# Order of TensorE's products in the split feed-forward up blocks: four wide then four narrow, against wide and narrow in turn

## The reference, cut to what matters

```
D_MODEL = 1024
SEQ = 256
D_FF = -(-8 * D_MODEL // (3 * 256)) * 256
...
def swiglu(h, w13, w2):
    a, b = jnp.split(h @ w13, 2, axis=-1)
    return (jax.nn.silu(a) * b) @ w2
```

## Time and profile before

| | |
|---|---|
| time, three runs | 1642.73, 1645.28 and 1645.38 us, median 1645.28 us |
| profiled execution | span 1643.5 us from the first to the last instruction; its own time is not listed apart from the three runs |
| TensorE products | 1585.3 us, 96% of the span |
| TensorE weight loads | 1365.7 us, 83% |
| VectorE | 1135.1 us, 69% |
| ScalarE | 728.8 us, 44% |
| GpSimd | 285.9 us, 17% |
| line 912, 512 columns | 1440 products, and as many loads |
| line 916, 256 columns | 1440 products, and as many loads |

### The profile page before, as it was taken

One profiled execution on the slowest core, in us unless ns is written; L12 is line 12 of the kernel. 1 busy time (PEld: TensorE's weight loads), 2 busy tenths in 40 slices (PEclk: granted clock), 3 DMA queues, 4 the chain that ended last, 5 costly groups with the idle time before them and its releaser, 6 DMA issues.

```text
span 1643.5 us, 29379 instructions
## 1 busy us (share of the span) xinstructions
PE 1585.3 (96%) x11682; PEld 1365.7 (83%) x11682; DVE 1135.1 (69%) x1815; ACT 728.8 (44%) x1077; POOL 285.9 (17%) x332
## 2 busy tenths in 40 slices
PE   4999988999999999999999999999999999999998
PEld 3998778786888888888996888888888898698887
DVE  5886456475687867887667568875878766755554
ACT  4444433403444354443556444445344445644443
POOL 0441445032400000000025000000000002400000
PEclk8999999999999999999999999999999999999999
DMA  9963100376778838785740588766787562164531
GB/s 374 373 243 128 52 3 4 122 281 247 293 300 328 332 129 343 298 330 227 247 155 2 189 332 335 302 265 232 300 336 297 232 216 105 57 241 162 224 155 63
DMA packets 60454, 363.84 MB, mean 221 GB/s; under 512 B 14017, under 2 KB 14785, under 8 KB 40513
## 3 DMA queue, kind: packets, MB, share of 16 engines
q1 hardware_dynamic: 60352, 362.42, 57.7%
HBM read 361.32 MB, written 1.08 MB: 221 GB/s over the span
## 4 chain that ended last, share of the span: by engine, by line
PE 83%; DVE 8%; DMA 3%; issue 3%; ACT 2%; POOL 1%; SPq 0%; POOLq 0%; DVEq 0%; ACTq 0%
PE psum L912 20%; PE psum L916 10%; PE psum L931 5%; PE psum L932 5%; PE psum L930 5%; PE psum L874 4%; PE psum L1412 2%; PE psum L1087 2%; PE psum L1358 2%; PE psum L1382 2%; PE psum L983 2%; PE psum L1383 1%; PE psum L1384 1%; DMA arena<-in_ada_head 1%; DMA ring<-in_in 1%
## 5 line engine op out<-in xcount | busy, mean ns | idle before, releaser
L912 PE MATMUL psum<-split 128*128 128x512 f32 x1440 | 392.6, 394 | 0.0
L2052 DVE TENSOR_TENSOR split<-ring,split 128x2048 fp32r<-128x2048 f32 x100 | 229.3, 2297 | 173.5 <-ACT split L1589 170.1
L912 PEld LDWEIGHTS psum<-split 128*128 128x128 f32 x1440 | 249.1, 189 | 35.2
L1589 ACT ACTIVATE split<-ring 128x2048 fp32r<-128x2048 f32 x100 | 190.4, 1909 | 182.1 <-PE psum L916 91.2
L916 PEld LDWEIGHTS psum<-split 128*128 128x128 f32 x1440 | 220.8, 189 | 30.4
L916 PE MATMUL psum<-split 128*128 128x256 f32 x1440 | 229.0, 281 | 0.0
L2739 POOL TENSOR_TENSOR scratch<-scratch 128x512 f32<-128x512 f32 x45 | 58.3, 1296 | 773.1 <-ACT scratch L1614 773.1
L2021 DVE CUSTOM_DVE_ANT_0 arena<-arena,c_row 128x1024 f32<-128x1024 f32 x144 | 167.6, 1220 | 0.0
L932 PE MATMUL psum<-split 128*128 128x512 f32 x400 | 156.6, 392 | 0.0
L931 PE MATMUL psum<-split 128*128 128x512 f32 x400 | 156.6, 391 | 0.0
L930 PE MATMUL psum<-split 128*128 128x512 f32 x400 | 156.1, 390 | 0.0
(11 more groups left out here) (457 smaller groups left out, 3210.4 us busy)
## 6 DMA issues: line engine op xcount, KB each, us to landing
ring<-in_up SPq DMA_DIRECT2D x55, 2048.0 KB, 10.0
arena<-in_ada SPq DMA_DIRECT2D x168, 512.0 KB, 6.4
ring_down<-in_down SPq DMA_DIRECT2D x55, 1024.0 KB, 4.9
ring<-in_in SPq DMA_DIRECT2D x18, 2048.0 KB, 9.9
ring<-in_gates SPq DMA_DIRECT2D x4, 2048.0 KB, 8.8
arena<-in_ada_head SPq DMA_DIRECT2D x4, 1536.0 KB, 17.3
ring_down<-in_w_out SPq DMA_DIRECT2D x3, 2048.0 KB, 11.6
ring<-in_w_out SPq DMA_DIRECT2D x3, 2048.0 KB, 9.3
```

Source lines behind the costliest of these rows:

```text
L912: mm(bank[4 + j], up_hi[:, h, a], h_both[:, kt_].rearrange("p s n -> p (s n)"), start=(kt_ == 0), stop=(kt_ == KD - 1), skip_group_check=True)
L1589: F(up_hi[:, h], ring[:, (g + c) % 2, h * 2048:(h + 1) * 2048], ACT.Copy).then_inc(up_high, 1)
L2052: tt(up_lo[:, h], ring[:, (g + c) % 2, h * 2048:(h + 1) * 2048], up_hi[:, h].bitcast(F32), ALU.subtract).then_inc(up_low, 1)
```

## The change

In each block the two loops over the four pieces become one: the 512-column product of a piece is followed at once by the 256-column product of the same piece. Nothing else differs; number, operands and sizes of products and loads are as before, and so are the waits and the signals.

```diff
                             for k in range(4):
                                 a, kt_ = slice(k * 512 + j * P, k * 512 + j * P + P), 4 * h + k
                                 mm(bank[4 + j], up_hi[:, h, a], h_both[:, kt_].rearrange("p s n -> p (s n)"),
                                    start=(kt_ == 0), stop=(kt_ == KD - 1), skip_group_check=True)
-                            for k in range(4):
-                                a, kt_ = slice(k * 512 + j * P, k * 512 + j * P + P), 4 * h + k
                                 last = mm(bank[4 + j][:, 0:S], up_lo[:, h, a], h_hi[:, kt_], start=False, stop=(kt_ == KD - 1), skip_group_check=True)
                         last.then_inc(half_done, 1)
```

## The result

The changed kernel takes 1649.45 us (median of 16 runs), the kernel before 1644.12 us beside it; the ratio is 1.0029, with a 95% interval from 1.0021 to 1.0038. So it is slower by 4.8 us (3.5 to 6.2) by this ratio, which is taken from all runs; the two medians lie 5.3 us apart. 5.5 us less were forecast. The time lies in the range of 1630 to 1650 us, but on the side that had a chance of 0.18.

The account below looks back on a forecast made before the run. TensorE, never waiting, was taken as the bound, through distances between product starts. 45 runs going from 11.21 to 11.08 us gave 5.9 us less, written as 5.5: 1645.3 - 5.5 = 1639.8 us, range 1630 to 1650 us.

Parts of the forecast that it names:

- What bounds the stage: TensorE's wide and narrow products: nothing is waited for, time is the distances between starts; about 504 of 1643.5 us.
- I take the unmixed price, 346.2 ns: Alternating wide and narrow products settle at their uniform prices, 226.2 + 120.0 ns a pair, against 350.3; 5.9 us less.
- The down product: Behind each run: still starts behind a narrow product, so its slow first eleven products stay, 2 us in all.
- No settling: Rival: the order only shuffles the same losses, a pair stays at 350 ns, 0 us, 1645 us; chance 0.30.
- The slower rival: A penalty at each change from narrow to wide: 352.5 to 355 ns a pair, 3.2 to 6.8 us more; chance 0.18.
- The larger gain: Rival: the wide product covers the narrow one's load, a pair falls toward 338 ns, 9 to 17.7 us less; chance 0.12.
- No change by the formula of the Trainium skill's page: Warm products cost columns at 2.4 GHz plus 2.5 ns in any order: 325 ns a pair, 0 us; no chance given.

Follow-up runs that it names:

- two and two: Two wide products, then two narrow ones, in turn, against the four and four of the kernel before; ratio 0.9967, 5.4 us less.
- lead_two: The changed kernel, but the first block of each half goes two wide, two narrow; ratio to the kernel before 0.9972, 4.6 us less.
- half_narrow: The changed kernel with only the narrow product's load cut to 64 weight columns, half of that product's rows left out; 340 ns a pair in the timeline shown.
- groups of sixteen: All sixteen wide products of a half, then its sixteen narrow ones, against the kernel before; ratio 0.9964, and 0.9964 again on another chip.
- thirty-two: All thirty-two wide products of a chunk over both halves, then the thirty-two narrow ones, against the kernel before; ratio 0.9971.

## Why the prediction was wrong, step by step

**What bounds the stage** was right: no wait came in, and 45 chunks at 0.106 us are the whole result. So were the count of products, the clock of 1.00, and that other engines take no part.

**The step that failed is "I take the unmixed price, 346.2 ns".** It measured 353.3, where 350.3 was the price before. Its reason, that a pattern which repeats has time to settle, was half right: the alternation settles by its third pair, but at a beat of its own, 7 ns above the sum of its parts. The runs show that one sequence has at least two such beats, 347 and 353, and that entry from the settled products of the down product leads to the dearer one, whichever width comes first.

**The down product** was held to stay the same but for "these 2 us ... the most that moves". It went from 5.487 to 5.503 us, 45 x 0.016 = 0.7 us, part of the 4.8: inside that bound, but a loss.

**No settling**, 350 ns a pair and 0 us, is excluded by the 353.3 ns and by the interval of the ratio.

**The slower rival** had the right bounds (352.5 to 355 ns, 3.2 to 6.8 us) and thus the right time for this entry. A penalty fixed to each change from narrow to wide, its mechanism, is not what the runs bear out: two and two makes twice the changes of before and is faster, and `lead_two` pays 347 for one and one.

**The larger gain** named the narrow product's own load, the one that runs beside the wide product ahead. With full loads no run came under 346 ns a pair; with that load and its output halved (`half_narrow`) a pair is at 347 ns, or at 340, by the entry. The order did not hide the full load.

**No change by the formula of the Trainium skill's page (TensorE: Matmul & The Clock Gate, Back-to-back issue gap)** falls: order and entry alone move a pair between 347 and 353 ns. That section gives the formula for an isolated product, and says that in a stream of loads and products both set the distance; the prediction left that out.

What inside TensorE holds the state from one product to the next stays open; no row names it.

## What to carry to other kernels

Where TensorE runs back to back, the distance between products of unlike width need not be the sum of their uniform prices: it belongs to the sequence and to how it is entered, so read it from a trace of that very sequence, several entries of it, before an order is changed. Long uniform stretches did well here: groups of sixteen gave 0.36%, twice measured. The next step to thirty-two gave nothing more, and brought a wait in. Two and two (0.33%) and the led alternation (0.28%) came close. When a rearrangement of equal work moves the time by a few tenths of a per cent and no wait has come in, look for a repeating cycle of distances.

## What the runs showed of the hardware that was not expected

The same alternating products, on the same engine with no wait between them, repeat at 347 or at 353 ns a pair. All 40 runs behind a down product took the dearer beat in the changed kernel's trace. In `lead_two` the alternation took the other one in all 40 of these runs in one trace and in 39 of 40 in the second; the fortieth began behind a wait of 0.74 us. Runs of chunk two, entered from another stretch, take either. The distances don't depend on banks, token columns or the weights' addresses (1.06 us for three pairs in all three runs), but do on the number of weight columns: with 64 in place of 128 for both products a pair costs 340 ns. With 64 columns one and one is cheaper than four and four (340 against 343 ns), where the changed kernel with 128 is dearer than before (353 against 350); at the beat of 347, though, one and one is the cheaper with 128 as well. In all these one-and-one kernels of 512 and 256 columns three pairs settle at 1.02, 1.04 or 1.06 us, 20 ns apart; why, no run shows.
